# Transposing q and k first in the fp32 group of a unit, and evacuating them first on ACT, in a two-layer hybrid encoder

## The reference

```python
h = rms_norm(x, ln_g) * (1 + scale) + shift
A: qa, ka = rope(rms_norm(q)), rope(rms_norm(k))     # 4 heads, each two maps of width 64
   w  = softmax(s[0]) - lam * softmax(s[1]);  ya = rms_norm(w @ va) * (1 - lam_init)
B: neighbourhood attention on the token grid, 8 heads of 64, learned position bias
C: dilated windows, 12 heads of 128 in 3 groups, mixed by their softmax denominators
merged = sum_i sigmoid(h @ Wg_i) * ((y_i * silu(h @ Wz_i)) @ w_br[i])
x = x + gate * (merged @ w_out)
```

## Time and profile before

| | |
|---|---|
| median of 3 runs | 2479.88 us (2478.91 to 2481.21) |
| the profiled execution | 2480.99 us |
| its span, first to last instruction | 2479.1 us |
| mean granted TensorE clock | 0.991 |
| PE busy | 2391.6 us, 96% |
| PEld busy | 2156.1 us, 87% |
| DVE busy | 1415.8 us, 57% |
| ACT busy | 1029.1 us, 42% |
| POOL busy | 94.3 us, 4% |

### The profile page before, as it was taken

The page is one execution under the profiler, slowest core; times in us unless marked ns, Lnnn a source line. Parts: engine busy times, 40 slices in busy tenths (PEclk is TensorE's granted clock), DMA queues, the critical chain, the costliest instruction groups (busy, mean ns, idle before and its releaser), DMA issues.

```text
span 2479.1 us, 38434 instructions
## 1 busy us (share of the span) xinstructions
PE 2391.6 (96%) x14514; PEld 2156.1 (87%) x14514; DVE 1415.8 (57%) x4051; ACT 1029.1 (42%) x2738; POOL 94.3 (4%) x141
## 2 busy tenths in 40 slices
PE   2899999999999999999979999999999999999999
PEld 1788888889899999988868888888988999998888
DVE  1887523685336767652468874267743677765432
ACT  2666523564224444341245663156431444444220
POOL 1210000110000000000020100011000000000000
PEclk9899999999999999999999999999999999999999
DMA  6111112111211110231331112211121111122113
GB/s 265 51 59 69 58 63 83 64 54 61 76 51 52 52 52 28 91 102 60 104 111 45 40 35 77 71 46 59 33 79 64 39 52 52 52 77 86 65 59 124
DMA packets 39079, 171.17 MB, mean 69 GB/s; under 512 B 5104, under 2 KB 9840, under 8 KB 36976
## 3 DMA queue, kind: packets, MB, share of 16 engines
q1 hardware_dynamic: 30832, 150.68, 17.9%
q10 hardware_dynamic: 8064, 18.03, 2.0%
HBM read 162.40 MB, written 6.29 MB: 68 GB/s over the span
## 4 chain that ended last, share of the span: by engine, by line
PE 92%; DVE 3%; ACT 2%; DMA 1%; ACTq 1%; issue 1%; DVEq 0%
PE ps_proj L573 76%; PE ps_pv L680 3%; PE ps_pt L655 3%; PE ps_score L642 3%; PE ps_score L633 2%; PE ps_pv L674 1%; PE ps_tr L695 1%; PE ps_tr L696 1%; DVE normed L1142 1%; DMA col<-in_cols 1%; PE ps_proj L593 1%; DVE act_lo L1133 0%; ACTq L996 0%; ACT w_hi L793 0%; PE ps_tr L687 0%
## 5 line engine op out<-in xcount | busy, mean ns | idle before, releaser
L573 PE MATMUL ps_proj<-w_hi,act_hi 128*128 128x384 f32 x1920 | 666.9, 347 | 23.9 <-POOL act_lo L554 14.6
L573 PE MATMUL ps_proj<-w_lo,act_hi 128*128 128x384 f32 x1920 | 646.3, 337 | 0.0
L573 PE MATMUL ps_proj<-w_hi,act_lo 128*128 128x384 f32 x1920 | 646.1, 336 | 0.0
L573 PE MATMUL ps_proj<-act_hi,w_hi 128*128 128x512 f32 (+1 forms) x1408 | 477.1, 339 | 12.1 <-DVE act_lo L1370 6.1
L573 PE MATMUL ps_proj<-act_lo,w_hi 128*128 128x512 f32 (+1 forms) x1408 | 475.5, 338 | 0.0
L573 PE MATMUL ps_proj<-act_hi,w_lo 128*128 128x512 f32 (+1 forms) x1408 | 474.5, 337 | 0.0
L573 PEld LDWEIGHTS ps_proj<-w_hi,act_hi 128*128 128x128 f32 x1920 | 363.3, 189 | 25.6 <-issue 15.7
L573 PEld LDWEIGHTS ps_proj<-w_lo,act_hi 128*128 128x128 f32 x1920 | 363.8, 189 | 0.0
L573 PEld LDWEIGHTS ps_proj<-w_hi,act_lo 128*128 128x128 f32 x1920 | 362.7, 189 | 0.0
L573 PEld LDWEIGHTS ps_proj<-act_hi,w_hi 128*128 128x128 f32 x1408 | 268.0, 190 | 42.5 <-DVE prod L1313 7.3
L573 PEld LDWEIGHTS ps_proj<-act_hi,w_lo 128*128 128x128 f32 x1408 | 267.8, 190 | 28.6
(11 more groups left out here) (148 smaller groups left out, 3177.0 us busy)
## 6 DMA issues: line engine op xcount, KB each, us to landing
w_raw<-in_w SPq DMA_DIRECT2D x128, 768.0 KB, 4.3
w_raw<-in_w SPq DMA_DIRECT2D x40, 512.0 KB, 4.2
w_ada<-in_w_mod SPq DMA_DIRECT2D x11, 1536.0 KB, 6.3
first_ada<-in_w_first SPq DMA_DIRECT2D x4, 2048.0 KB, 14.8
out_y<-merged ACTq DMA_DIRECT2D x16, 384.0 KB, 4.7
merged<-in_x_in ACTq DMA_DIRECT2D x8, 384.0 KB, 29.0
x_old<-in_x_in ACTq DMA_DIRECT2D x8, 384.0 KB, 5.5
x_old<-out_y ACTq DMA_DIRECT2D x8, 384.0 KB, 5.2
```

The source lines that it names most:

```text
L573: op = pe.matmul(out, sta[s](k), mov[m](k), start=(k == 0 and n == 0), stop=(k == chunks - 1 and n == 2))
```

## The change

turn_unit(u2) goes from the end of the fp32 group to its head, ahead of scores(a0); turn_out(u2) on ACT goes from behind copy_probs(a1) to right behind rstds(u1), ahead of turn_out_y(a3) and exps(a0); the list of events of ps_tr has q and k ahead of y in each group.

```diff
@@ turned_events
     for n, u in enumerate(UNITS):
+        if n >= 2 and UNITS[n - 2][0] in "qa":
+            out.append(("t", UNITS[n - 2]))
         if n >= 3 and OPENED[n - 3] is not None and OPENED[n - 3][1] == "A":
             out.append(("y", OPENED[n - 3]))
-        if n >= 2 and UNITS[n - 2][0] in "qa":
-            out.append(("t", UNITS[n - 2]))
@@ PE, between
                     if k == 1:
+                        if u2 is not None and u2[0] in "qa":
+                            turn_unit(u2)
                         if a0 is not None:
                             scores(a0)
                         if a3 is not None and a3[1] == "A":
...
                         if a1 is not None:
                             turn_probs(a1)
-                        if u2 is not None and u2[0] in "qa":
-                            turn_unit(u2)
@@ ACT
                 if u1 is not None and u1[0] == "q":
                     rstds(u1)
+                if u2 is not None and u2[0] in "qa":
+                    turn_out(u2)
                 if a3 is not None and a3[1] == "A":
                     turn_out_y(a3)
                 if a0 is not None:
...
                 if a1 is not None:
                     copy_probs(a1)
-                if u2 is not None and u2[0] in "qa":
-                    turn_out(u2)
```

## The result

| | before | changed |
|---|---|---|
| median, same chip | 2480.18 us (4 runs) | 2495.8 us (4 runs, 2494.25 to 2498.7) |
| ratio | 1 | 1.0065, interval 1.0047 to 1.0082 |
| profiled execution / its span | 2480.99 / 2479.1 | 2498.7 / 2496.9 |
| ratio in a second comparison | 1 | 1.0051, interval 1.0039 to 1.0064 |

The change costs time: 12.9 us (2494.45 against 2481.51) or 15.6 us (2495.8 against 2480.18) in medians. The forecast was 9.3 us dearer, 2489.2. The direction was right. The first median lies above the band of 2484.5 to 2494 that was given 0.62 and just inside the wide range (up to 2496), and the forecast itself is 3.6 to 6.3 us too small.

What follows compares the result with a forecast made beforehand. PE was taken to bound the kernel (92% of the last chain). Terms 3.3+2.0+2.8+0.8+0.4 = 9.3 us took the median from 2479.88 to 2489.2; range 2484.5 to 2494 (chance 0.62), wide range 2480 to 2496.

Steps and rivals of the forecast that it cites:

- the formula: Branch A, y's transpose: PE can go on at L913's end plus 0.34; no stop if L913 ends by 0.94 or 0.52.
- Sample tiles: Branch A, sample tiles behind a weight copy or DVE's low part: a stop of 0.49 in four, +2.0 us.
- The seams: PE's steps between neighbouring matmuls: sum 0.38 before and after, so nothing; ends -8 and +6 us over 87 groups.
- The cover of the moved copy: ACT, ahead of the exponentials: its 114.4 us wait for DVE's maxima hides the 0.37 us copy, costed at nothing.
- Rival 1: Branch A, stop at 1390.56: ACT keeps ahead, 4.7 us of old stops go, 2475.2 us; chance 0.05.
- Rival 2: No change: ACT's lead adds up, or PE's wait for the first gate absorbs stops before z; +3, 2483; chance 0.18.
- Rival 3: Layers 1 and 0: no catching up, each late group pays in full; +18, 2498 us; chance 0.12.
- Rival 4: PE's clock falls behind six stops of about 1 us, 2 us a stop; +12 on the forecast, 2501; chance 0.03.
- The runs of layer 1: Branch A, three runs at tiles 3 to 5 of a head, where weights come twice on end: +2.8 us.
- C's first groups: C's first group of each layer, where qk comes short at the head: 0.2 each, +0.4 us.
- Groups without scores: Branch A, six groups with no scores between q, k and y: 0.85 instead of 0.22, less two old stops; +3.3 us.
- Layer 0: Six groups behind an "a" unit or its neighbour -0.2, at 174.71 +0.4, the next group +0.6: together +0.8 us.

Runs made afterwards that it cites:

- experiment 5: The changed kernel with one more 0.37 us ACT copy ahead of that of q and k in groups with y: 2500.62 us, 1.0076 to the kernel before.
- experiment 6: Against the kernel before, PE turns q and k first only in groups without y, ACT's copy of them stays last: 2486.78 us, 1.0022.

## Why the prediction was right and where it was wrong

**Right: the direction and the mechanism.** One wait went, another came, ACT's L913 sets when the copy can be made, and PE now reaches the second writer 0.86 or 1.28 us behind the head of the group, where it took up to 2.56 before (1380.18 to 1382.74). The earlier trace rows gave the formula, and it holds to 0.02 us at the stop shown. For the two groups of the earlier trace rows it forecast a stop of 1.03 and then 1.0 against 1.18 today; measured are +1.16 (+0.67 against the second profile of the kernel before, which loses 0.49 there without the change) and -0.20. The other two runs, forecast at 0.9 and 1.0, gave 0.94 and 1.0. Sample tiles: 2.0 and 2.05. The seams were put at zero out of a range of -8 to +6, and are zero; that was in part luck, since the 0.20 was taken from another form of matmul. The cover of the moved copy held (ACT still waits 91.9 us for the maxima).

**Rivals.** Rival 1 (ACT ahead) fell at once. Rival 2 (+3) fell with branch A's 11 us; the stops before z are not absorbed. Rival 3 (no catching up, +18) fell in layer 1, by experiment 5, and is true of the three pairs of layer 0 behind an "a" unit. Rival 4 (the clock) fell: 1.00 around the stop of 1.16, and at all 21 stops before y. "HAM oscillation — how this bites in real kernels" of "TensorE: Matmul & The Clock Gate" in the Trainium skill tells of a kernel whose bursts of matmuls are shorter than the waits for a transfer between them, and whose next burst then starts at the low clock. The prediction made of it that each new stop would cost again what it stops. That goes beyond the page: stops of 0.3 to 1.2 us with 4 us of work and more between them are not its case, and they don't speak against it. The 3.05 us ahead of 2424.84, with a granted clock of 0.64 in the next 4.2 us, agree with it.

**The step that failed** is one assumption under several terms: that the other engines keep their place. With q and k at the head, scores, values and probabilities all start 0.22 later and so stand 0.2 to 0.3 us nearer to the next group's head. The prediction set that 0.22 against ACT's wait for the maxima alone ("this cover stays and the tail of ACT's iteration loses 0.37"). But DVE's maxima follow the scores, with qk and the sum of squares behind them, and ACT's square of pv follows the values. It shows at four places, and at the first it is only a part.

**The runs of layer 1** (2.8 forecast, 3.5 measured). The group ahead of the two of the earlier trace rows, DVE's timeline of before, where PE's scores start at 1373.12:

```profile
1371.68 0.93 DVE L1275 SCALAR_TENSOR_TENSOR probs<-probs,mix 128x512 f32<-128x512 f32 x1
...
1372.85 0.40 DVE L1158 TENSOR_REDUCE ssq<-square 128x4 f32<-128x256 f32 x1
```

of the kernel before in its second profile, with the scores at 1372.92:

```profile
1371.67 1.27 DVE L1275 SCALAR_TENSOR_TENSOR probs<-probs,mix 128x512 f32<-128x512 f32 x1
...
1373.19 0.40 DVE L1158 TENSOR_REDUCE ssq<-square 128x4 f32<-128x256 f32 x1
```

and of the changed kernel, where q starts at 1385.34 at the same place of the unit:

```profile
1384.38 1.29 DVE L1275 SCALAR_TENSOR_TENSOR probs<-probs,mix 128x512 f32<-128x512 f32 x1
...
1385.91 0.40 DVE L1158 TENSOR_REDUCE ssq<-square 128x4 f32<-128x256 f32 x1
```

L1275 starts 0.96 ahead of the head instead of 1.44 and takes 1.29 instead of 0.93; L1158 starts 0.57 behind the head instead of 0.27 ahead of it. L913 follows L1158, ends at 1.55 instead of 0.71 (1373.62+0.21), so 0.6 beyond the limit of 0.94: the stop at 1387.21 that the prediction had not listed, 0.51 to 0.60 us. That is nearly the whole of the difference in the three runs.

Only a part of it comes from the change. In the second profile of the unchanged kernel L1275 is as long (1.27), and L913 ends 1.25 behind the head (1373.96+0.21 less 1372.92). By the prediction's formula that row would have given a stop of 0.3. What is left in L913's end, 0.3 in the first profile of the changed kernel and 0.4 in the second (1.67), is about the scores' later start, 0.31 behind q, which is the head now. L1275 is long only where GpSimd works beside it:

```profile
1384.29 2.05 POOL L542 TENSOR_TENSOR bias<-rel_s,mask_b_sb 128x256 f32<-128x256 f32 x2
```

It starts 0.09 ahead of L1275 here and 0.33 behind L1275's start in the first profile of before (1372.01). In that profile L1275 takes 0.75 in 31 of its 32 rows of this size and 0.93 in this one. So the prediction read the place from one profile, and the other profile of the same kernel has it half a microsecond later. Both profiles of the changed kernel have L1275 long; whether the change makes that likelier, two profiles of each can't tell.

**C's first groups** (0.4 forecast, 1.1 measured) are the same step. DVE before, then the changed kernel, DVE and PE:

```profile
526.82 0.42 DVE L1209 TENSOR_TENSOR qk<-gained,newton 128x256 f32<-128x256 f32 x1
...
535.60 0.42 DVE L1209 TENSOR_TENSOR qk<-gained,newton 128x256 f32<-128x256 f32 x1
...
536.17 0.30 PE L695 MATMUL ps_tr<-ident,qk 128*128 128x128 f32 x1 [0.34 <-DVE qk L1209]
```

Before, qk was written 0.04 behind the head (526.82+0.42 against scores at 527.20), and its price had been taken from there, 0.2 with the restart. It is now 0.36 behind it (536.02 against 535.66, where q would have started): 0.3 later, of which the scores' 0.22 is the greater part.

**Groups without scores** are not that step, but a term taken too small: 0.67 instead of 0.55 on average (4.0 for 3.3). At the "a" unit of the changed kernel:

```profile
159.72 0.33 PE L695 MATMUL ps_tr<-ident,qk 128*128 128x128 f32 x1
159.89 0.27 PE L696 MATMUL ps_tr<-ident,qk 128*128 128x128 f32 x1
160.20 0.38 ACT L856 ACTIVATE qkv<-ps_tr 128x256 f32<-128x256 f32 x1 [0.39 <-PE ps_tr L696]
160.63 0.33 PE L687 MATMUL ps_tr<-ident,y_tok 128*128 128x128 f32 x1 [0.47 <-ACT qkv L856]
```

From q to y is 0.91, forecast 0.85: q to k is 0.17 behind the modulation's matmuls, not 0.11. The rest is mainly the two old stops of 0.23 that were taken off the sum and do not show.

**Layer 0** (0.8 forecast, 1.6 measured) is the step again: each of three pairs of groups behind an "a" unit is 0.77 dearer and then 0.40 cheaper, where the forecast had about zero; at 174.71 it is 0.6 instead of 1.0. ACT before, with the next group's scores at 161.06:

```profile
159.44 0.37 ACT L946 ACTIVATE square<-ps_pv,rden 128x128 f32<-128x128 f32 x1 [0.53 <-PE ps_pv L680]
...
161.10 1.48 ACT L793 ACTIVATE w_hi<-w_raw 128x1536 fp32r<-128x1536 f32 x1
```

and in the changed kernel, with q at 163.19:

```profile
161.90 0.37 ACT L946 ACTIVATE square<-ps_pv,rden 128x128 f32<-128x128 f32 x1 [0.54 <-PE ps_pv L680]
...
163.30 1.47 ACT L793 ACTIVATE w_hi<-w_raw 128x1536 fp32r<-128x1536 f32 x1
...
165.05 0.39 ACT L856 ACTIVATE qkv<-ps_tr 128x256 f32<-128x256 f32 x1
```

L946 waits for PE's values in both, 1.62 ahead of the next head before and 1.29 now. So the 0.28 that the moved copy frees behind L922 is gone again: L793 starts 0.11 behind the head instead of 0.04, where the forecast had it 0.24 ahead. Three times 0.35 is 1.0 of the 1.3 that the six groups cost more than forecast. And since L946 stands behind the new stop of the "a" unit, nothing of that stop comes off in the next group: the pair whose "a" unit has no y, and no stop, costs the same 0.77.

**C's second z units** (nothing forecast, 0.21 each) are the same step too. PE's next unit waits there for DVE's product with the gate, which follows ACT's L902, and ACT comes to L902 behind its copy of the values (L883). Before, with the group's head at 1072.62, and in the changed kernel, with it at 1082.19:

```profile
1073.71 0.28 ACT L883 ACTIVATE y_t<-ps_pv 128x128 f32<-128x128 f32 x1 [5.65 <-PE ps_pv L680]
...
1077.14 0.50 PE L573 MATMUL ps_proj<-act_hi,w_hi 128*128 128x512 f32 x1 [0.64 <-DVE prod L1313]
```

```profile
1083.96 0.28 ACT L883 ACTIVATE y_t<-ps_pv 128x128 f32<-128x128 f32 x1 [0.82 <-PE ps_pv L680]
...
1086.92 0.50 PE L573 MATMUL ps_proj<-act_hi,w_hi 128*128 128x512 f32 x1 [0.85 <-DVE prod L1313]
```

The values wait their turn behind the six small matmuls and L883 starts 1.77 behind the head instead of 1.09. ACT's copy of the small matmuls (L862), which stood last, is out of the way by then, so L902 comes 0.21 later, and PE stands 0.21 longer.

**Costed at nothing, wrongly, and open**: C's other groups, 1.1 us in both layers. "B and C the same to 0.1 us in all" fell. The cause of the 0.03 us per group in C is open: experiment 6 puts it with PE's order; the matmuls of the fp32 group are as long as before, and the steps of the projection behind it are 0.175 to 0.185 for some of 0.173.

By terms, then: 9.3 forecast, 13.7 measured; of the 4.4 missing, 0.7 are groups without scores, 0.7 the runs of layer 1, 0.8 layer 0, 0.7 C's first groups, 0.4 the z units and 1.1 the other groups of C. The failed step is 0.3 of the runs, layer 0, C's first groups and the z units, about 2.2 and half of it all.

## What to carry to other kernels

When two writers share one buffer and its reader's time is set by other work, swapping them or moving them apart moved the stop in all four orders measured here, and none was without one; a second buffer removed it. When a step is moved to the head of a stretch, everything behind it comes nearer to the next head: give that time to every engine whose chain starts there, not only to the one whose wait you look at. An engine's lateness comes off only where its chain begins ahead of the new stop. And read a place on which a term rests in two profiles of the kernel: here they had L913's end half a microsecond apart.

## What the runs showed of the hardware that had not been expected

- The seams between forms of matmul are even in the sum: projection to scores on half of the array's rows 0.27 and a transpose to a transpose 0.11 before, projection to transpose 0.175 and transpose to these scores 0.20 now, 0.38 either way. The order of the forms does not matter here.
- Stops of 0.3 to 1.2 us, 21 of them, leave the granted clock at 1.00, the 2.4 GHz level, also where two of 1.16 and 0.90 stand 7.6 us apart. So does a stop of 1.39 us at a load of weights. Stops of 3.04 and 3.05 us were followed by 0.50 over 2.8 us and 0.64 over 4.2 us.
- DVE's L1275 (128x512, fp32) took 0.75 us in 30 or 31 of its 32 rows of a profile, and 0.93 to 1.29 in the one or two that ran beside GpSimd's L535 or L542.
- The fp32 group's place costs 0.03 us in groups of C in which nothing waits. It stays open.
- Two profiles of one kernel differ by 1.65 us in the stop at a late load of weights and by up to 1.5 us at the start of the output, but by 0.05 us in nearly all other units. A difference of 1 us at such a place is no finding; one of 0.2 us in a plain unit mostly is.
